# v of block 2 in two halves of 512 columns, each from two pairs of weight tiles held together

## What is computed

```python
for i in range(DEPTH_2):                       # 2 layers
    h = rms_norm_2(x, attn_norm[i])
    if i % N_MIXERS == 0:                      # layer 0
        mix = stick_breaking_mixer(h, w_in[i], w_out[i])      # 16 heads of 64
    else:                                      # layer 1
        mix = diff_mixer(h, positions, w_in[i], w_out[i], ...)  # 8 heads of 128, rope, softmax
    x = x + mix
    x = x + swiglu_ffn(rms_norm_2(x, ffn_norm[i]), w_gate[i], w_up[i], w_down[i])

q, k, v = jnp.split(jnp.einsum('bsd,de->bse', h, w_in), 3, axis=-1)   # in both mixers, e = 3 x 1024
```

## Time and profile before

| what | value |
|---|---|
| time, median of 3 runs | 2141.3 us (2139.76 to 2141.69) |
| profiled execution: span from the first to the last instruction | 2147.6 us |
| profiled execution's own time beyond that | not given apart from the span |
| mean granted clock of TensorE | 0.996 |
| TensorE busy | 2104.2 us, 15046 matmuls |
| DVE, ACT, POOL busy | 1257.7, 1063.8, 237.1 us |
| block 2, layer 0: q0 to the output projection's last matmul | some 890 to 1160 us |
| block 2, layer 1: the same | some 1528 to 1784 us |

### The profile page before, as it was taken

How to read it: one execution, slowest core, us unless ns; L and a number is a source line. 1 busy time by engine, 2 the same in 40 slices (tenths; PEclk the granted TensorE clock), 3 DMA queues, 4 the chain that set the end, 5 groups by cost and what they waited for, 6 DMA issues and landing times.

```text
span 2147.6 us, 36021 instructions
## 1 busy us (share of the span) xinstructions
PE 2104.2 (98%) x15046; PEld 1680.3 (78%) x15046; DVE 1257.7 (59%) x2218; ACT 1063.8 (50%) x2094; POOL 237.1 (11%) x240
## 2 busy tenths in 40 slices
PE   7999999999999999999999999999999999999999
PEld 6777877887777887877777888888777778888887
DVE  6777667667755456655567543445577775443442
ACT  6666756666655236656665332233455554222331
POOL 0123221312310010100001000000100001000000
PEclk9999999999999999999999999999999999999999
DMA  5321112121214332211112232222212212232222
GB/s 181 108 81 65 70 66 90 66 78 61 71 51 167 132 137 79 71 67 60 59 40 84 98 102 94 99 98 98 84 64 64 65 59 98 98 103 94 98 100 77
DMA packets 36227, 186.89 MB, mean 87 GB/s; under 512 B 4560, under 2 KB 4944, under 8 KB 16992
## 3 DMA queue, kind: packets, MB, share of 16 engines
q1 hardware_dynamic: 36064, 184.58, 25.0%
HBM read 173.00 MB, written 7.90 MB: 84 GB/s over the span
## 4 chain that ended last, share of the span: by engine, by line
PE 89%; DVE 5%; ACT 4%; issue 1%; DMA 1%; SPq 0%; POOL 0%; DVEq 0%; ACTq 0%
PE ps L1887 88%; PE ps L1890 1%; ACT arena L2839 1%; DVE spl L2345 1%; ACT spl L2842 1%; ACT hh L2839 1%; DVE x L2705 0%; DMA raw<-wstream 0%; DVE hl L2656 0%; DVE arena L2364 0%; DVE arena L2648 0%; DVE x L2634 0%; DVE arena L2630 0%; DMA arena<-spill 0%; ACT pad L2839 0%
## 5 line engine op out<-in xcount | busy, mean ns | idle before, releaser
L1887 PE MATMUL ps<-hh,spl 128*128 128x512 f32 (+1 forms) x3152 | 1021.0, 397 | 10.1 <-ACT x L2842 2.2
L1887 PEld LDWEIGHTS ps<-hh,spl 128*128 128x128 f32 x3152 | 585.6, 189 | 144.6 <-issue 17.3
L1887 PE MATMUL ps<-hl,spl 128*128 128x512 f32 (+1 forms) x1568 | 616.5, 393 | 0.0
L2345 DVE TENSOR_TENSOR spl<-raw,spl 128x512 fp32r<-128x512 f32 x596 | 422.4, 733 | 168.4 <-ACT spl L2842 167.4
L1887 PE MATMUL ps<-arena_r,spl 128*128 128x512 f32 x1968 | 466.9, 391 | 8.8 <-DVE arena_r L2357 8.5
L1887 PEld LDWEIGHTS ps<-arena_r,spl 128*128 128x128 f32 x1968 | 369.8, 188 | 88.7 <-issue 10.9
L2842 ACT ACTIVATE spl<-raw 128x512 fp32r<-128x512 f32 x596 | 345.1, 619 | 143.5 <-PE ps L1887 138.3
L1887 PEld LDWEIGHTS ps<-hl,spl 128*128 128x128 f32 x1568 | 295.8, 189 | 59.8 <-issue 4.3
L1887 PE MATMUL ps<-arena 32*32 32x32 f32 (+5 forms) x5664 | 218.4, 225 | 11.0 <-issue 10.9
L2839 ACT ACTIVATE arena<-arena 128x512 f32<-128x512 f32 (+3 forms) x204 | 132.3, 650 | 183.7 <-DVE arena L2710 141.1
L1887 PEld LDWEIGHTS ps<-arena 32*32 32x32 f32 (+4 forms) x5664 | 127.6, 117 | 86.8 <-issue 74.7
(11 more groups left out here) (272 smaller groups left out, 2151.5 us busy)
## 6 DMA issues: line engine op xcount, KB each, us to landing
raw<-wstream SPq DMA_DIRECT2D x148, 1024.0 KB, 4.9
arena<-spill SPq DMA_DIRECT2D x17, 256.0 KB, 5.3
GS<-g_rows SPq DMA_DIRECT2D x16, 256.0 KB, 3.7
spill<-x SPq DMA_DIRECT2D x14, 256.0 KB, 2.0
arena<-arena SPq DMA_DIRECT2D x18, 128.0 KB, 2.0
x<-xT SPq DMA_DIRECT2D x4, 512.0 KB, 6.4
spill<-arena SPq DMA_DIRECT2D x8, 256.0 KB, 2.0
x<-xT SPq DMA_DIRECT2D x1, 2048.0 KB, 7.2
```

The costliest lines, as they stand in the source:

```text
L1887: return pe.matmul(out, lhsT, rhs, start=start, stop=stop, skip_group_check=True)
L2345: tt(spl[:, p % 2, 1, c], raw[:, p % 2, c], spl[:, p % 2, 0, c].bitcast(F32), ALU.subtract) \
```

## The change

Each half of v (512 columns, all 8 K blocks) is made from two consecutive pairs: the first holds K blocks 0 to 3, the second K blocks 4 to 7, 512 columns of each. For token blocks 0 and 1, and then for 2 and 3: 4 K blocks of the first pair for one token block and the other, then 4 of the second. Both main banks and both slots of `spl` are thus in use at once. A matmul has 512 moving columns. The halves stand behind m = 0 and 4 in layer 0, and behind m = 1 and 5 in layer 1. `v_out` copies 512 columns at a time. The second pair is split during the first token block, the pair after it during token block 2 of the second pair. The waits on v follow the halves (m // 4).

```diff
--- before.py
+++ after.py
@@ -20,7 +20,7 @@
 EARLY = 6
 HEAD_STREAM = ("dn_z", "dn_q", "att_q", "att_z", "dn_v", "dn_k", "early")
 OUT_FIRST = 4
-V_BEHIND = ((0, 2, 4, 6), (1, 3, 5, 7))
+V_BEHIND = ((0, 4), (1, 5))
 LAM_INIT = 0.8 - 0.6 * math.exp(-0.3)
 MAGIC = 12582912.0
 TWO_PI = 2.0 * math.pi
@@ -51,7 +51,7 @@
 PE_H, DV_H, AC_H = 0.44, 0.41, 0.37
 HOP = 0.08
 CHANGE = 0.088
-ONE_PASS = ("mul", "tok", "ar_ss", "cv_r", "on_b", "st_w", "st_t")
+ONE_PASS = ("mul", "tok", "vmm", "ar_ss", "cv_r", "on_b", "st_w", "st_t")
 TAIL_32 = 0.4
 MARGIN = 0.0
 SLACK = 1.0
@@ -347,24 +347,34 @@
     def gemm_tok(op, done):
         o.flush()
         p, b = divmod(o.block, 16)
-        assert b == 0
-        for tb in range(4):
-            if tb == 1:
-                split(p + 1)
-            o.until(main.ready)
-            u = main.take()
-            o.clock["PE"] = max(o.clock["PE"], u.t, o.pair_t[p])
-            for q in range(4):
-                st = o.main("tok", p, tb, q, cost=[("PE", 0.72)])
-                st.u, st.op, st.p, st.tb, st.q = u, op, p, tb, q
-                st.need = None if tb else [op.ready[k] for k in (2 * q, 2 * q + 1) if k not in op.seen]
-                op.seen |= {2 * q, 2 * q + 1}
-                if q < 3:
+        assert b == 0 and all(k in op.seen for k in range(KT))
+        for tbs in ((0, 1), (2, 3)):
+            us = {}
+            for half in range(2):
+                for tb in tbs:
+                    if half == 0:
+                        o.until(main.ready)
+                        us[tb] = main.take()
+                    u = us[tb]
+                    o.clock["PE"] = max(o.clock["PE"], u.t, o.pair_t[p + half])
+                    for k in range(4):
+                        if (tb, half) == (0, 0):
+                            split(p + 1, [k])
+                        if (tb, half) == (2, 1):
+                            split(p + 2, [k])
+                        st = o.main("vmm", p + half, tb, k, cost=[("PE", 3 * MUL)])
+                        st.u, st.op, st.p, st.tb, st.half, st.k = u, op, p + half, tb, half, k
+                        st.pair_mark = (half, tb, k) == (0, 3, 3)
+                        if k < 3:
+                            o.step()
+                    if half == 1:
+                        done(tb, u)
+                    elif tb == 3:
+                        o.n_pair_marks += 1
+                        o.pair_done[p] = ("pairs", o.n_pair_marks)
                     o.step()
-            done(tb, u)
-            o.step()
-        o.pair_done[p] = ("bank", u)
-        o.block += 16
+        o.pair_done[p + 1] = ("bank", u)
+        o.block += 32
 
     def low(op, k, kind, *key, then=None):
 
@@ -1181,7 +1191,7 @@
             main.give(st.u)
 
         def done(tb, u):
-            st = o.main("v_out", layer, tb, j, cost=[("AC" if tb % 2 else "DV", 0.4)])
+            st = o.main("v_out", layer, tb, j, cost=[("AC", AC_B) if tb % 2 else ("DV", DV_B)])
             st.u, st.tb, st.j, st.layer = u, tb, j, layer
             main.give(u)
         gemm_tok(h, done)
@@ -1363,7 +1373,7 @@
                 t_f = o.now
             o.now = t_x
             yield "PE"
-            while ("v_out", 0, kb, m // 2) not in o.at or not obs.ready():
+            while ("v_out", 0, kb, m // 4) not in o.at or not obs.ready():
                 yield "PE"
             uo = obs.take()
             st = o.add("st_o", m, kb, cost=[("PE", 0.1 + 0.86 * f)], u=uo)
@@ -1510,7 +1520,7 @@
             return
         qk.give(iqk, o.at["df_s", m, 3])
         yield "AC PE"
-        while ("v_out", 1, 3, m // 2) not in o.at or not obk.ready() or not on_slot.ready():
+        while ("v_out", 1, 3, m // 4) not in o.at or not obk.ready() or not on_slot.ready():
             yield "AC PE"
         _, on_old = on_slot.take()
         o.behind(on_old)
@@ -1529,7 +1539,7 @@
     ob = Operand("os_lo", "ob_h", "ob_l")
     for m in range(KT):
         o.spawn("score", score_lane(m))
-        behind = [("df_out", m)] + [("br_out", "k", 7)] * (m > 2) + [("v_out", 1, 3, 3)] * (m == 7)
+        behind = [("df_out", m)] + [("br_out", "k", 7)] * (m > 2) + [("v_out", 1, 3, 1)] * (m == 7)
         o.spawn("split", split_lane("ob", ob, m, behind))
     for m in range(KT):
         o.until(qk.ready)
@@ -1933,6 +1943,21 @@
                         mm(o, hi[:, c], wl[:, k, :], False, False)
                         i = mm(o, lo[:, c], wh[:, k, :], False, k == 7)
                     if q.q == 3:
+                        i.then_inc(filled[u.b], 1)
+                elif kind == "vmm":
+                    u, j, c = q.u, q.p % 2, slice(q.tb * 128, q.tb * 128 + 128)
+                    if q.k == 0 and q.half == 0 and u.n > 1:
+                        w.wait_ge(drained[u.b], u.n - 1)
+                    w.wait_ge(sem("w_lo"), 4 * q.p + q.k + 1)
+                    n = slice(512 * q.k, 512 * q.k + 512)
+                    hi, lo = HI[q.op.hi][4 * q.half + q.k], HI[q.op.lo][4 * q.half + q.k]
+                    o = psum[u.b][:, :]
+                    mm(o, hi[:, c], spl[:, j, 0, n], q.half == 0 and q.k == 0, False)
+                    mm(o, hi[:, c], spl[:, j, 1, n], False, False)
+                    i = mm(o, lo[:, c], spl[:, j, 0, n], False, q.half == 1 and q.k == 3)
+                    if q.pair_mark:
+                        i.then_inc(sem("pairs"), 1)
+                    elif q.half == 1 and q.k == 3:
                         i.then_inc(filled[u.b], 1)
                 elif kind == "norm":
                     w.wait_ge(sem("norm_add"), 7)
@@ -2260,8 +2285,8 @@
                         w.wait_ge(drained[u.b], u.n - 1)
                     t = at["st_w", m, kb].u
                     w.wait_ge(drained[t.b], t.n)
-                    if m % 2 == 0:
-                        t = at["v_out", 0, kb, m // 2].u
+                    if m % 4 == 0:
+                        t = at["v_out", 0, kb, m // 4].u
                         w.wait_ge(drained[t.b], t.n)
                     for b in range(2):
                         c = m * 128 + 64 * b
@@ -2305,8 +2330,8 @@
                     for j in range(4):
                         t = at["df_t", m, j].u
                         w.wait_ge(drained[t.b], t.n)
-                        if m % 2 == 0:
-                            t = at["v_out", 1, j, m // 2].u
+                        if m % 4 == 0:
+                            t = at["v_out", 1, j, m // 4].u
                             w.wait_ge(drained[t.b], t.n)
                     for kb in range(4):
                         i = mm(psum[u.b][:, kb * 128:S], v8[:, kb, m * 128:m * 128 + 128],
@@ -2659,7 +2684,7 @@
                 elif kind == "v_out" and q.tb % 2 == 0:
                     full(q.u)
                     empty(at["rs_col", q.layer].u)
-                    ts(v8[:, q.tb, q.j * 256:q.j * 256 + 256], psum[q.u.b][:, 0:256], rs_col[:, q.tb:q.tb + 1], None,
+                    ts(v8[:, q.tb, q.j * 512:q.j * 512 + 512], psum[q.u.b][:, :], rs_col[:, q.tb:q.tb + 1], None,
                        ALU.mult).then_inc(drained[q.u.b], 1)
                 elif kind == "st_q":
                     m = q.key[0]
@@ -3088,7 +3113,7 @@
                         if k > 2:
                             w.wait_ge(sem("br_out"), 16)
                         if k == 7:
-                            full(at["v_out", 1, 3, 3].u)
+                            full(at["v_out", 1, 3, 1].u)
                     copy(HI[name + "_h"][k], o8[k]).then_inc(sem("os_hi"), 1)
                 elif kind == "re_hi":
                     which, k = q.key
@@ -3178,7 +3203,7 @@
 
                 elif kind == "v_out" and q.tb % 2:
                     full(q.u)
-                    f(v8[:, q.tb, q.j * 256:q.j * 256 + 256], psum[q.u.b][:, 0:256], ACT.Identity,
+                    f(v8[:, q.tb, q.j * 512:q.j * 512 + 512], psum[q.u.b][:, :], ACT.Identity,
                       scale=rs_col[:, q.tb:q.tb + 1]).then_inc(drained[q.u.b], 1)
                 elif kind == "st_e":
                     z = at[("st_z",) + q.key]
@@ -3429,7 +3454,9 @@
                 fm(w, 128 * m)
                 fm(w, 1024 + 128 * m)
             if m in V_BEHIND[i]:
-                tm(w, 2048 + 256 * V_BEHIND[i].index(m), 1)
+                c = 2048 + 512 * V_BEHIND[i].index(m)
+                for k in range(0, 8, 4):
+                    out.append(w[128 * k:128 * k + 512, c:c + 512].reshape(4, 128, 512).transpose(1, 0, 2).reshape(128, 2048))
         fm(a["w_out_2"][i], 0, 8, 0, OUT_FIRST)
         for j, k in last_behind(2):
             fm(a["w_out_2"][i], 128 * j, 1, k, k + 1)
```

## The result

| | us |
|---|---|
| before, median of the runs timed beside after | 2141.5 (2139.8 to 2145.0) |
| after, median of 4 runs | 2169.9 (2169.4 to 2171.0) |
| ratio, 95% interval | 1.0127 (1.0116 to 1.0139) |
| span of the profiled execution, after | 2168.3 |

The change makes the kernel 28.5 us slower. The forecast was 4.9 us slower; its range ended at 2152.5.

The account below looks back on a forecast made before the run. TensorE, busy for 98% of the span, was taken as the bound: − 4.3 (wider matmuls) + 6.0 (split of ob[3]) + 1.5 (layer 0's slot) + 1.7 (clock) = + 4.9, so 2146.2 us; range 2136.5 to 2152.5.

Parts of the forecast that it names:

- Wider matmuls: v projections in block 2: 384 matmuls of 512 columns replace 768 of 256, a gain of 4.3 us (3.9 to 5.0).
- Evictions and weight tiles: v's PSUM copies and weight-tile splits in block 2 stay covered by other work; costed at nothing.
- The split of ob[3]: End of layer 1: output projection waits before its fourth K block for k7's last rope, 6.0 us uncovered (2.4 to 9.8).
- rival (a): End of layer 1: enough side matmuls, 10.9 us for 4.4, cover the wait; only the gain is left, 2137.0 us; 15%.
- Heads 5 and 6 stand to k7 as before: Layer 1: no v lies between these heads and k7 in either kernel, so their relative timing was taken as unchanged.
- Head 7's block just fits: Layer 1's output projection: 47.4 us of TensorE time before this block's first use, against a 45.6 us chain; nothing added.
- Layer 0, the slot: Layer 0: q4 waits until head 1's last score block frees one of three q/k slots; 1.5 us, from 0 to 6.
- The clock: End of layer 1: TensorE's granted clock falls once after waiting, adding 1.7 us (0 to 3.4).
- Rival (c): Both attention stages wait: layer 0 6 us, layer 1 9.8, clock falls twice (3.4), gain 3.9; 2156.6 us; 13%.

Follow-up runs that it names:

- pos_only: Against after: v in the narrow 256-column quarters and single weight tiles of before, two in a row at after's places; 2176.7 us, ratio 1.0158.
- ob41: After, with the splits of layer 1's attention-output blocks 3 to 5 in tiles of their own, not waiting for k7's rope; 2171.8 us, ratio 1.0142.
- first_only: Before's 256-column quarters, with only the second quarter moved ahead in each layer, next to the first; 2157.7 us, ratio 1.0076 to before.
- last_only: Before's 256-column quarters, with only the fourth quarter moved ahead in each layer, next to the third; 2157.5 us, ratio 1.0071 to before.
- slots4: After, with a fourth set of q/k tiles in layer 0, so that head 4 need not wait for head 1; 2170.7 us, ratio 1.0139.
- filler: After, with five added matmuls on a tile of zeros at TensorE's waits at the end of layer 1; 2168.6 us, ratio 1.0116.
- late1: After, with the second half of v one block of q and k later in both layers; 2170.3 us, ratio 1.0131.
- less_after: After, without the hidden-upper by weights-lower product in the second half of layer 1's v, 7.3 us less TensorE work; 2170.2 us, ratio 1.0113.
- short_after: After, with two DVE operations of each softmax block of layer 1 working on only 64 columns; 2170.2 us, ratio 1.0131.

## Why the prediction was wrong

The sign was right and the size was not: 28.5 us in place of 4.9. Step by step:

- *Wider matmuls*, −4.3. The pace was right (0.228 for 0.229). The work of the three stretches fell by 1.0 only; 2.5 us are the width (rest, pos_only to after), and about 1.5 are given back by the new order (before to pos_only), whose origin I haven't found. The medians give the width 6.6 ± 4, so 4.3 may stand. The other rule that I weighed, an estimate of 1.0 us from the isolated gap of the Trainium skill (TensorE: Matmul & The Clock Gate, Back-to-back issue gap), is below both values.
- *Evictions and weight tiles*, 0. Right: in after no v matmul with hh waits, and the trios keep their pace.
- *The split of ob[3]*, +6.0. The wait stands where it was forecast, behind the ninth matmul of the output projection, and TensorE is idle there for 6.58 us. The size is right by luck: two errors cancel. k7's rope, the wait that I had named, was done after 10.8 us, in time for a split at 13; the split came at 20.2, since on ACT it stood behind head 6's output block, which ran at half clock. And the side work let in was 17.2 − 6.6 = 10.6 us (4.8 of them lost by the clock), where I had counted 4.4: that is nearly what rival (a) asked for, and TensorE waited all the same, since these steps wait for one another. *Heads 5 and 6 stand to k7 as before* was the false premise. Without v behind k7 head 6's output block starts 10.6 us behind k7's last matmul (1743.37 − 1732.73) and not 25.6: it comes into this stretch, ahead of the split of ob[3], which I had not counted.
- *Head 7's block just fits*, 0. Right in after, where nothing waits for it. It was as narrow as said: ob41 has 3.55 us there. From k7's last matmul to the first use of that block it is 53.3 us (before: 53.7), with 11.5 us of v less in it.
- *Layer 0, the slot*, +1.5. The mechanism was right. So were the times of the k blocks: k1 came out of PSUM 14 us later than before (13 forecast), k3 78 us behind the start of the layer (76 to 80). The wait was 0.98 + 4.44 us, near the upper bound of 6; taking a value near the low end was the error, and I had put no fall of the clock on it (1.3 us in after). first_only has it too, last_only hasn't, and slots4 removed it.
- *Layer 0, the rest of it*, not in the sum. This is the step that is missing altogether. I had worked out what taking v from behind m = 2 and 6 does to the slots, and not what m = 6 without its quarter does to the end of the layer: 3.5 us idle there, and 3.0 us of clock in after. last_only has the same three waits and first_only none, so this is the last quarter's move and not the late start of head 1. In layer 1 the first move was at nothing in the same way (idle +4.4 us ahead of the output projection; first_only has +3.3, last_only +0.1).
- *The clock*, +1.7. It was 10.5 us. I had granted one fall of one window; it fell behind the slot wait and at the end of layer 0, and at the end of layer 1, there at 1.2 GHz for three windows of 5 us. filler shows cause and price at the last place. The Trainium skill (TensorE: Matmul & The Clock Gate, HAM oscillation) has pauses between bursts of matmuls drop the clock; the runs agree, but its case has waits for DMA of 3 to 5 us, and here a series of waits of 0.8 to 2.4 us for DVE and ACT was enough.

The misses add up: idle in layer 0 +7.1 (8.6 for 1.5), idle in layer 1 ahead of the projection +4.4, behind it +0.6, clock +8.8, work +3.3: 24.2, and 4.9 + 24.2 = 29.1.

Rival (c), both stages wait, came nearest with 2156.6: both waits and more than one fall of the clock are there. The end of layer 0 is not in it either. All of my cases had the same fault. Each wait was worked out from one chain and its local cover, as if the rest of the order stood still. What the change moves is 11.5 us of projection at a time, out of a stretch in which several heads wait for round trips. The heads' round trips stay, and with less to do between them TensorE waits for each. That waits, once removed, turn up elsewhere (slots4, ob41, late1), and that neither less TensorE work nor less DVE work helps much (less_after, short_after), fits this and nothing else that I tried. That the places cost the time, each of the two moves about half of it, is shown; that no order could have avoided it is not. All those kernels with less work kept the planner's order, and a new order for the shorter work was not tried. Nor was the rival that the planner's order is at fault: in after it has the split of ob[3] behind head 6's output block on ACT, although the rope was done 6.5 us before ACT came to it, and the same places with that one step put ahead were not run. ob41 comes nearest, and there the wait stood at head 7's block instead.

## What to carry to other kernels

Where independent work fills the gaps of serial chains, a block of it that is moved can cost most of its length at the place it leaves, however busy the engine is on average: here 46 us of v, moved ahead by two blocks of q and k, cost 33 us. Price such a move by the stretch that loses the cover, all its chains together, not by the one wait that can be named; and before widening a matmul, look whether the wider piece can stay where the narrow ones were. Where a wait is expected on TensorE, count the clock too: it cost half as much again as the idle time.
